# Experts of a mixture-of-experts layer taken four at a time instead of two at a time

## The chip, the cores and the metric

The kernel runs on one core of one Trainium2 chip. The metric is the device time of one launch in microseconds (us). Before the change the median of three runs is 1275.25 us (1270.68 to 1278.07). The engines are TensorE (PE; PEld is its weight load), VectorE (DVE), ScalarE (ACT), GpSimd (POOL) and SyncE (SP), which here only issues transfers.

## The reference, cut to what matters

384 tokens (128 context, 256 latent) pass two layers, each a token mixer (attention, then a long convolution) and a mixture of 32 experts. The experts are what the change touches:

```python
g_idx = argmax(t @ wg + bg)                     # one of 4 groups
e_val, e_idx = top_k(logits of its 8 experts, 2)  # two experts per token
combine = one_hot(expert_id) * weight           # 384 x 2 = 768 (token, expert) rows
a, b = t @ w_gate[e], t @ w_up[e]               # 1024 -> 256
out += (silu(a) * b * combine[e]) @ w_down[e]   # 256 -> 1024
```

All is float32. An expert has 3 MB of weights (gate and up 1 MB each, down 1 MB), a layer 96 MB. Only the rows that an expert was chosen for have to be computed. Counted from the reference on the inputs of the measurement, the experts 0 to 31 get these many rows:

- layer 0: 7 16 1 26 | 18 0 27 11 | 25 5 33 24 | 71 21 11 80 | 13 1 15 55 | 18 28 9 7 | 32 29 55 60 | 14 7 26 23.
- layer 1: 76 24 2 47 | 19 54 2 2 | 51 13 27 20 | 44 31 8 12 | 19 20 4 13 | 27 32 26 25 | 31 4 21 32 | 23 17 25 17.

## The kernel before

**Expert stage.** A layer's 32 experts are taken as 16 pairs. 128 slots stand on the partitions: 64 for one expert of the pair, 64 for the other (`WIN = 64`). In order, a pair does this: its 128 token rows are brought to `G` by an indirect DMA of POOL (the first two pairs: by matrix products with a 0/1 matrix, L825), PE turns them (L832) into `GT`, whose halves ACT (L1207) and DVE (L1627) copy out of the banks; PE multiplies with gate and up (`gate_up`, L849: 8 steps over the inner dimension, 2 experts each, every product 64 stationary columns against 512 moving ones, so that two stand side by side in the array); ACT takes silu (L1230), DVE the weighted product (L1655); PE turns it (L855), DVE copies it (L1658), and PE multiplies with down (L863). ACT (L1238) and DVE (L1667) copy the result to `Y`, and POOL scatters its rows to memory (L1811). In the trace one product stands as two MATMUL records.

**Further windows.** Where an expert of a pair has more than 64 rows, the pair is computed again for slots 65 to 128 and so on (`extra`, L869 to L892 on PE): every engine loads two counts into registers, compares and branches; if there is a window, the whole chain (turn, gate and up, silu, turn, down, copy, scatter) runs through serially, ahead of the pair's first window. By the counts above three pairs have one: experts 12/13 (71), 14/15 (80) in layer 0, 0/1 (76) in layer 1. That is 32 + 3 = 35 passes.

**Weights.** The 12 MB `ring` holds two pairs of 6 MB, each of three 2 MB transfers (gate, up, down). SP issues gate and up of pair q+2 when `gate_up` of pair q has ended (semaphore `gu_mm`, which also follows the pair's further windows) and down when the down product has ended (`dn_mm`).

**Filter work.** During layer 0's experts the kernel also computes the filters of the next mixer, one of eight per two pairs: PE products `taps` (L582), `spectra` (L599 to L604) and `sizes` (L613), written out by hand between the products of the pairs, with copies on DVE and ACT, sums on POOL (L1872), small loads by SP (L391 to L394) and a 768 KB store by ACT for each.

After the last scatter SP loads all expert rows back (L429), and the residual sum and the norm follow.

## Time and profile before

| | us |
|---|---|
| median of 3 runs (lowest, highest) | 1275.25 (1270.68, 1278.07) |
| the profiled execution's own time | 1280.37 |
| its span, first to last instruction | 1278.5 |
| PE busy | 1089.1 (85%) |
| DVE, ACT, POOL busy | 476.8, 257.0, 185.4 |
| moved by DMA | 324.54 MB |

Busy time counts a stretch once however many matrix products overlap in it; the mean of one record is longer than its share of the busy time where products stand side by side. The experts of layer 0 run from about 315 to 627 us of the span, those of layer 1 from about 970 to 1239 us.

### The profile page before, as it was taken

The numbers are of one execution on the slowest core, as the hardware profiler recorded it, in microseconds if no ns is written. First come the engines' busy times: TensorE is split into PE (matmuls) and PEld (weight loads), VectorE is DVE, ScalarE is ACT, GpSimd is POOL, SyncE is SP. The second block draws the span as 40 slices with busy tenths as digits, with TensorE's granted clock in tenths as the row PEclk, the third lists the DMA queues.
The fourth block names the chain that finished last, engine by engine and source line by source line (L and its number), as shares of the span: only waits on it lengthen the run. The fifth ranks groups of instructions, "written<-read, shape, count | busy, mean of one in ns | idle before, by whom it ended". The sixth has DMA issues, their size and how long they took to land.

```text
span 1278.5 us, 14637 instructions
## 1 busy us (share of the span) xinstructions
PE 1089.1 (85%) x5429; PEld 574.4 (45%) x5429; DVE 476.8 (37%) x1014; ACT 257.0 (20%) x498; POOL 185.4 (15%) x209
## 2 busy tenths in 40 slices
PE   5799888987999789999879999989765988878864
PEld 3344555555444234443345565658662422222223
DVE  3355556234233113332263336784540111111116
ACT  2211334022333123223231110000221000000001
POOL 1020000002322023221100002130011222222100
PEclk8899989986999899999889999999967989889997
DMA  9996985532899569999870200505320899999943
GB/s 351 404 322 264 251 294 225 227 132 70 313 395 401 228 238 356 398 406 410 305 286 1 99 1 0 230 1 198 154 94 20 325 413 413 413 412 407 407 161 129
DMA packets 94241, 324.54 MB, mean 254 GB/s; under 512 B 17647, under 2 KB 33423, under 8 KB 77380
## 3 DMA queue, kind: packets, MB, share of 16 engines
q1 hardware_dynamic: 71936, 303.49, 61.3%
q0 software_dynamic: 15504, 13.37, 3.4%
q10 hardware_dynamic: 6708, 6.45, 1.4%
q8 instruction: 58, 0.95, 0.3%
q14 instruction: 35, 0.29, 0.1%
HBM read 333.22 MB, written 30.11 MB: 284 GB/s over the span
## 4 chain that ended last, share of the span: by engine, by line
PE 63%; DMA 19%; DVE 7%; issue 4%; ACT 3%; SPq 3%; POOL 0%; ACTq 0%; another core or an unknown queue 0%; POOLq 0%; DVEq 0%
PE bank L849 15%; DMA ring<-in_moe_w_up 10%; PE bank L997 10%; PE bank L863 6%; PE bank L668 3%; PE bank L1036 3%; PE bank L784 3%; DMA ring<-in_w_ada 3%; DMA hT<-in_hy_log_decay 3%; PE bank L564 3%; PE bank L599 2%; PE bank L1025 2%; PE bank L983 2%; DMA ring<-in_moe_w_down 2%; PE bank L796 2%
## 5 line engine op out<-in xcount | busy, mean ns | idle before, releaser
L849 PE MATMUL bank<-ring,work 128*64 128x512 f32 x1120 | 267.5, 633 | 44.3 <-issue 38.2
L849 PEld LDWEIGHTS bank<-ring,work 128*64 128x64 f32 x1120 | 82.5, 145 | 220.6 <-issue 216.4
L863 PE MATMUL bank<-ring,work 128*64 128x512 f32 x560 | 129.4, 604 | 4.3 <-DVE work L1643 1.5
L997 PE MATMUL bank<-hT,ring 128*128 128x384 f32 x384 | 128.0, 494 | 5.3 <-ACT hT L1134 5.3
L1655 DVE SCALAR_TENSOR_TENSOR work<-bank,work 128x256 f32<-128x256 f32 x32 | 15.5, 484 | 261.3 <-ACT work L1230 248.6
L997 PEld LDWEIGHTS bank<-hT,ring 128*128 128x128 f32 x384 | 74.0, 194 | 58.0 <-issue 9.7
L863 PEld LDWEIGHTS bank<-ring,work 128*64 128x64 f32 x560 | 37.5, 138 | 74.1 <-issue 63.4
L1230 ACT ACTIVATE work<-bank 128x256 f32<-128x256 f32 x32 | 12.3, 383 | 249.8 <-PE bank L849 249.8
L1667 DVE COPY work<-bank 128x512 f32<-128x512 f32 x32 | 22.1, 692 | 106.8 <-PE bank L863 106.8
L1806 POOL DMA_INDIRECT work<-token_vectors,work x28 | 28.7, 1026 | 199.6 <-PE bank L832 185.7
L564 PE MATMUL bank<-ring,condS 128*32 128x256 f32 x768 | 48.6, 408 | 10.0 <-DVE ada L1334 5.5
L1811 POOL DMA_INDIRECT expert_rows<-work x32 | 32.0, 1000 | 114.9 <-DVE work L1667 113.0
L599 PE MATMUL bank<-hT,const 128*128 128x256 f32 x160 | 43.8, 409 | 4.6 <-DVE hT L1365 4.6
L1036 PE MATMUL bank<-work,ring 128*128 128x128 f32 (+1 forms) x256 | 42.2, 327 | 1.7 <-DVE work L1757 1.7
L668 PE MATMUL bank<-hT,ring 128*64 128x384 f32 x256 | 43.0, 489 | 0.0
L784 PE MATMUL bank<-work,ring 128*128 128x384 f32 x128 | 41.5, 487 | 0.7 <-DVE work L1499 0.7
L1270 ACT ACTIVATE work<-bank,pc 128x128 f32<-128x128 f32 (+1 forms) x48 | 17.6, 418 | 119.8 <-PE bank L997 119.8
L1238 ACT ACTIVATE work<-bank 128x512 f32<-128x512 f32 x32 | 19.1, 598 | 111.5 <-PE bank L863 111.5
L1036 PEld LDWEIGHTS bank<-work,ring 128*128 128x128 f32 x256 | 38.4, 190 | 5.5 <-issue 2.1
L1729 DVE TENSOR_SCALAR work<-work,pc 128x385 f32<-128x385 f32 x24 | 11.5, 480 | 76.6 <-ACT work L1270 76.6
L1125 ACT ACTIVATE sq<-xT 128x384 f32<-128x384 f32 x38 | 19.7, 522 | 100.9 <-DVE xT L1421 59.2
L564 PEld LDWEIGHTS bank<-ring,condS 128*32 128x32 f32 x768 | 24.8, 116 | 33.4 <-DVE ada L1334 9.0
(269 smaller groups left out, 1481.5 us busy)
## 6 DMA issues: line engine op xcount, KB each, us to landing
ring<-in_moe_w_gate SPq DMA_DIRECT2D x32, 2048.0 KB
ring<-in_moe_w_up SPq DMA_DIRECT2D x32, 2048.0 KB
ring<-in_moe_w_down SPq DMA_DIRECT2D x32, 2048.0 KB
ring<-in_w_ada SPq DMA_DIRECT2D x24, 2048.0 KB, 12.5
ring<-in_hy_w_in SPq DMA_DIRECT2D x6, 2048.0 KB, 20.4
filter_spectra<-work ACTq DMA_DIRECT2D x8, 768.0 KB
work<-expert_rows SPq DMA_DIRECT2D x16, 384.0 KB, 6.7
ring<-filter_spectra SPq DMA_DIRECT2D x2, 3072.0 KB, 12.1
```

The costliest lines, as they stand in the source:

```text
L564: last = mm(ada_bank(t)[32 * j:32 * j + 32, 0:256], condS[:, 4 * hk + k, :], w[:, k, 256 * j:256 * j + 256], start=(hk == 0 and k == 0), s ...
L599: last = mm(dst, m[:, off:off + P], smdf[:, part if part < 2 else r, c, :], start=(j == 0), stop=(j == len(ops) - 1))
L668: last = mm(bank[m % 2][b * HD:(b + 1) * HD, 0:T], wq[:, k, h * HD:(h + 1) * HD], hT[:, k, :], start=(k == 0), stop=(k == KD - 1))
L784: last = mm(bank[m % 2][:, 0:T], wo[:, k, m * P:(m + 1) * P], oT[:, k, :], start=(k == 0), stop=(k == KD - 1))
L796: last = mm(bank[c][:, 0:NG + NE], hT[:, k, c * P:(c + 1) * P], rout[:, l, k, :], start=(k == 0), stop=(k == KD - 1))
L849: last = mm(bank[2][WIN * j:WIN * (j + 1), :], gt[:, k, WIN * j:WIN * (j + 1)], gu[:, :, j, k, :], start=(k == 0), stop=(k == KD - 1))
L863: last = mm(bank[b + hf][WIN * j:WIN * (j + 1), :], AT[:, k, WIN * j:WIN * (j + 1)], dn[:, j, k, hf * HALF:(hf + 1) * HALF], start=(k == 0 ...
L983: last = mm(b[:, :], m[:, off:off + P], ztok[o][:, c, hf * HALF:(hf + 1) * HALF], start=(j == 0), stop=(j == len(ops) - 1))
L997: last = mm(bank[n % 2][:, 0:T], w[:, k, (n % 4) * P:(n % 4 + 1) * P], hT[:, k, :], start=(k == 0), stop=(k == KD - 1))
L1036: last = mm(bank[4 + m % 2][:, lo:hi], wout[:, k, m * P:(m + 1) * P], st[:, 2, k, a0:a1], start=(k == 0), stop=(k == KD - 1))
L1806: ind(out=G[:, q % 2, :], out_offset=None, in_=hD, in_offset=at_rows(tab[:, 4 * q + 1:4 * q + 2]), bounds_check=T - 1, oob_is_err=False).t ...
L1811: ind(out=yD, out_offset=at_rows(tab[:, 4 * q:4 * q + 1]), in_=Y[:, q % 2, :], in_offset=None, bounds_check=2 * T - 1, oob_is_err=False).t ...
```

## The change

The experts are taken as 8 quads of four, with 32 slots for each (`WIN = 32`). A product now has 32 stationary columns, and four stand side by side. The ring holds one quad in six units of 2 MB: gate and up of the first half of the inner dimension (units 0, 1), gate and up of the second half (2, 3), and the two inner halves of down (4, 5). SP issues units 0 to 3 of quad q+1 when PE has turned the activation of quad q (`at_mm`), units 4 and 5 when PE has turned the token rows of quad q+1 (`gt_mm`). A quad has a further window for each 32 rows, or part of 32, that its fullest expert has beyond 32. Up to two of them (`WOVEN = 2`) are woven in: their gate/up products stand between those of the first window and the turn of its activation, their down products after its down product. More than two would run in a serial loop (`rare`) ahead of the quad. The single buffers `G` and `Y` take the place of double ones.

By the counts, the quads of layer 0 have 0 0 1 2 1 0 1 0 further windows, those of layer 1 have 2 1 1 1 0 0 0 0: ten, and none goes to `rare`. That is 16 + 10 = 26 passes.

```diff
-PAIRS = NE // 2
-WIN = 64
+QUAD = 4
+QUADS = NE // QUAD
+WIN = P // QUAD
+WOVEN = 2
...
         def moe_loads(sp, l):
...
-            for q in range(2, PAIRS):
-                sp.wait_ge(S_("gu_mm"), B_("gu_mm") + q - 1)
-                load_gu(sp, l, q)
-                sp.wait_ge(S_("dn_mm"), B_("dn_mm") + 2 * (q - 1))
-                load_dn(sp, l, q)
-                if l == 0 and q % 2 == 1:
-                    load_filter(sp, q // 2)
+            for q in range(1, QUADS):
+                sp.wait_ge(S_("at_mm"), B_("at_mm") + q)
+                for i in range(4):
+                    load_unit(sp, l, q, i)
+                sp.wait_ge(S_("gt_mm"), B_("gt_mm") + 2 * (q + 1))
+                if l == 0:
+                    load_filter(sp, q)
+                for i in (4, 5):
+                    load_unit(sp, l, q, i)
...
+                def gate_up(gt, half):
+                    gu = half_gu(half)
+                    for k in range(KD // 2):
+                        kk = 4 * half + k
+                        for j in range(QUAD):
+                            last = mm(bank[2][WIN * j:WIN * (j + 1), :], gt[:, kk, WIN * j:WIN * (j + 1)], gu[:, :, j, k, :],
+                                      start=(kk == 0), stop=(kk == KD - 1))
+                    return last
...
+                def extra_gate_up(q):
+
+                    apart(pe)
+                    lo, hi = window_counts(q)
+                    with pe.If(hi > lo):
+                        pe.wait_ge(S_("xgath"), 16 * (lo + 1))
+                        turn_extra(0).then_inc(S_("xgt_mm"), 1)
+                        pe.wait_ge(S_("xgt_set"), 2 * (lo + 1))
+                        pe.wait_ge(S_("act_set"), B_("act_set") + q + 1)
+                        gate_up(GTx, 0)
+                        gate_up(GTx, 1).then_inc(S_("xgu_mm"), 1)
+                        apart(pe)
+                        with pe.If(hi > lo + 1):
...
-                for q in range(PAIRS):
-                    s = q % 2
-                    pe.wait_ge(sem(f"gu_in_{s}"), B_("gu_in") + 32 * (q // 2 + 1))
-                    copied(q)
...
+                for q in range(QUADS):
+                    pe.wait_ge(S_("gta_set"), B_("gta_set") + q + 1)
+                    pe.wait_ge(S_("gtb_set"), B_("gtb_set") + q + 1)
                     if q >= 1:
                         pe.wait_ge(S_("act_set"), B_("act_set") + q)
...
+                    rare(q)
+                    apart(pe)
+                    pe.wait_ge(sem("half_in0"), B_("half_in0") + 32 * (q + 1))
+                    gate_up(GT, 0)
+                    if l == 0 and q >= 1:
+                        for part in range(3):
+                            spectra(q - 1, part)
+                    pe.wait_ge(sem("half_in1"), B_("half_in1") + 32 * (q + 1))
+                    gate_up(GT, 1).then_inc(S_("gu_mm"), 1)
+                    extra_gate_up(q)
                     pe.wait_ge(S_("act_set"), B_("act_set") + q + 1)
-                    turn_act(S_("at_mm"))
+                    turn_act(A, S_("at_mm"))
+                    if l == 0:
+                        taps(q, 0)
+                        taps(q, 1)
...
+                    for hf in range(2):
+                        down(hf).then_inc(S_("dn_mm"), 1)
+                    if l == 0:
+                        taps(q, 2)
+                    extra_down(q)
+                    if q + 1 < QUADS:
+                        pe.wait_ge(S_("gath"), B_("gath") + 16 * (q + 1))
+                        for half in range(2):
+                            gather_turn(half)
+                    if l == 0 and q >= 1:
+                        sizes(q - 1)
```

On POOL, `extra_scatter(q)` waits until each further window's rows have landed before it goes on, and `extra_gather(q+1)` stands behind it; ACT and DVE got `extra_turned`, `extra_silu`, `extra_act` and `extra_rows`, each with its own loads of the two counts and its branch.

PE before, in layer 0: a pair's check (loads of `cumx`, compare), its further window, then the start of the pair's own work. L881 turns the window's rows, L849 is gate/up, L855 the turn of the activation, L863 down.

```order
L870 TENSOR_LOAD cumx
L870 ISA x2
L871 TENSOR_LOAD cumx
L871 ISA x2
L872 COMPARE_AND_BRANCH
L878 UNCONDITIONAL_BRANCH
L878 ISA
L881 MATMUL bank<-const,work 128x128 x8
L883 REGISTER_ALU
L849 MATMUL bank<-ring,work 64x512 x16
L855 MATMUL bank<-const,work 128x128 x2
L863 MATMUL bank<-ring,work 64x512 x8
```

PE after, in a quad of layer 0: the second half of the quad's own gate/up (L844), the check, two further windows (L862 turns rows), and only then the turn of the quad's activation (L850), whose semaphore lets SP load.

```order
L844 MATMUL bank<-ring,work 32x512 x16
L866 TENSOR_LOAD cumx
L866 ISA x2
L867 TENSOR_LOAD cumx
L867 ISA x2
L898 COMPARE_AND_BRANCH
L899 ISA
L862 MATMUL bank<-const,work 128x128 x8
L901 REGISTER_ALU
L844 MATMUL bank<-ring,work 32x512 x32
L906 COMPARE_AND_BRANCH
```

The further window went from ahead of the pair, where it was a chain to the end, to a place inside the quad; its down product moved behind the quad's own.

SP before, in layer 0, the loads of two pairs and the small loads of a filter:

```order
L399 DMA ring<-in_moe_w_gate 128x2x2048
L399 DMA ring<-in_moe_w_up 128x2x2048
L404 DMA ring<-in_moe_w_down 128x4x1024
L399 DMA ring<-in_moe_w_gate 128x2x2048
L399 DMA ring<-in_moe_w_up 128x2x2048
L404 DMA ring<-in_moe_w_down 128x4x1024
L391 DMA hT<-in_hy_log_decay 128x256
```

SP after, one quad:

```order
L408 DMA ring<-in_moe_w_gate 128x4x1024
L408 DMA ring<-in_moe_w_up 128x4x1024
L408 DMA ring<-in_moe_w_gate 128x4x1024
L408 DMA ring<-in_moe_w_up 128x4x1024
L397 DMA hT<-in_hy_log_decay 128x256
L399 DMA sq<-in_hy_filt_w 64x256
L400 DMA sq<-in_hy_filt_b 1x256
L397 DMA hT<-in_hy_log_decay 128x256
L399 DMA sq<-in_hy_filt_w 64x256
L400 DMA sq<-in_hy_filt_b 1x256
L413 DMA ring<-in_moe_w_down 128x4x1024 x2
```

The bytes are the same; 8 MB now start at one point and 4 MB at another, where six points stood for 12 MB, and a run of gate or up is 4 KB long where it was 8 KB.

DVE after, in a quad: the weighted product (L1731), then the check, and behind it the copy of the further window's turned rows (L1728).

```order
L1731 SCALAR_TENSOR_TENSOR work<-bank,work 128x256
L1723 TENSOR_LOAD cumx
L1723 ISA x2
L1724 TENSOR_LOAD cumx
L1724 ISA x2
L1757 COMPARE_AND_BRANCH
L1758 REGISTER_ALU
L1728 COPY work<-bank 128x512
L1731 SCALAR_TENSOR_TENSOR hd<-bank,work 128x256
```

Before, DVE made its check ahead of everything of the pair; now one stands between the product and the copy.

## Rows read from the trace of the kernel before

**Rows 1.** Windows: stretch, its length, busy us and instructions by engine, clock, DMA share, GB/s.
```profile
325.00:601.00 276.00, 260.00 (x1215) 111.89 (x1215) 81.34 (x119) 77.28 (x112) 68.62 (x77) 0.99 0.91 354
488.00:575.00 87.00, 86.83 (x407) 38.13 (x408) 29.51 (x42) 26.12 (x36) 27.08 (x29) 1.00 1.03 398
996.00:1227.00 231.00, 192.72 (x876) 69.92 (x876) 33.91 (x60) 23.32 (x44) 45.06 (x56) 0.93 1.00 404
```

**Rows 2.** Page: groups of instructions, busy us, mean ns of one, idle before.
```profile
L849 PE MATMUL bank<-ring,work 128*64 128x512 f32 x1120 | 267.5, 633 | 44.3 <-issue 38.2
...
L863 PE MATMUL bank<-ring,work 128*64 128x512 f32 x560 | 129.4, 604 | 4.3 <-DVE work L1643 1.5
...
L1655 DVE SCALAR_TENSOR_TENSOR work<-bank,work 128x256 f32<-128x256 f32 x32 | 15.5, 484 | 261.3 <-ACT work L1230 248.6
...
L1230 ACT ACTIVATE work<-bank 128x256 f32<-128x256 f32 x32 | 12.3, 383 | 249.8 <-PE bank L849 249.8
L1667 DVE COPY work<-bank 128x512 f32<-128x512 f32 x32 | 22.1, 692 | 106.8 <-PE bank L863 106.8
```

**Rows 3.** Timeline of PE: start, us, operation; 32-column products, one after an idle stretch.
```profile
27.02 3.66 PE L564 MATMUL bank<-ring,condS 128*32 128x256 f32 x64
36.77 5.57 PE L564 MATMUL bank<-ring,condS 128*32 128x256 f32 x64 [4.36 <-DVE ada L1334]
```

**Rows 4.** Timeline of PE, gate/up of pairs 3, 5, 6, 7 in layer 0.
```profile
367.30 7.09 PE L849 MATMUL bank<-ring,work 128*64 128x512 f32 x32
...
400.66 7.09 PE L849 MATMUL bank<-ring,work 128*64 128x512 f32 x32
...
438.54 7.09 PE L849 MATMUL bank<-ring,work 128*64 128x512 f32 x32 [1.02 <-DVE work L1646]
...
473.42 7.09 PE L849 MATMUL bank<-ring,work 128*64 128x512 f32 x32 [1.01 <-DVE work L1646]
```

**Rows 5.** Timeline, all engines, around the first check of layer 0.
```profile
308.22 0.31 DVE L1609 CAST cumx<-work 1x17 int32<-1x17 f32 x1
...
310.06 1.28 ACT L1230 ACT_TABLE_LOAD   x1 [2.04 <-issue]
```

**Rows 6.** Timeline of PE, first and last passes of the two layers.
```profile
314.92 9.89 PE L849 MATMUL bank<-ring,work 128*64 128x512 f32 x32 [4.85 <-issue]
...
621.34 5.15 PE L863 MATMUL bank<-ring,work 128*64 128x512 f32 x16 [0.52 <-DVE work L1658]
...
944.37 7.63 PE L825 MATMUL bank<-work 128*128 128x128 f32 x48 [3.70 <-DVE work L1579]
969.78 1.96 PE L881 MATMUL bank<-const,work 128*128 128x128 f32 x8 [17.77 <-DMA work<-token_vectors,curx]
...
1047.17 8.99 PE L849 MATMUL bank<-ring,work 128*64 128x512 f32 x32 [5.29 <-issue]
...
1235.52 3.65 PE L863 MATMUL bank<-ring,work 128*64 128x512 f32 x16 [0.52 <-DVE work L1658]
```

**Rows 7.** Timeline of SP: the first load of each layer's loop.
```profile
324.85 0.38 SPq L399 DMA_DIRECT2D ring<-in_moe_w_gate  x1
...
995.11 0.37 SPq L399 DMA_DIRECT2D ring<-in_moe_w_gate  x1
```

**Rows 8.** Timeline of POOL: gathers, and the instruction that waits for their landing.
```profile
443.46 1.04 POOL L1829 DMA_INDIRECT work<-token_vectors,curx  x1 [0.87 <-POOL curx L1826]
445.89 0.19 POOL L1837 COPY curx<-work 128x4 int32<-128x4 int32 x1 [1.40 <-DMA work<-token_vectors,curx]
...
966.31 1.01 POOL L1839 DMA_INDIRECT work<-token_vectors,curx  x1 [0.77 <-POOL curx L1837]
...
996.34 1.02 POOL L1839 DMA_INDIRECT work<-token_vectors,curx  x1 [0.78 <-POOL curx L1837]
1004.60 0.19 POOL L1837 COPY curx<-work 128x4 int32<-128x4 int32 x1 [7.25 <-DMA work<-token_vectors,curx]
```

**Rows 9.** Page: DMA issues, KB each, median us to landing (two in flight).
```profile
ring<-in_w_ada SPq DMA_DIRECT2D x24, 2048.0 KB, 12.5
```

More of the change, by code:

```diff
@@ L326, in build @@
         mtmp = [small(2, TC, NE) for _ in range(3)]
-        posk, rowk, wck, basek, wink, rowq = [small(2, TC) for _ in range(6)]
+        posk, rowk, wck, basek, wink = [small(2, TC) for _ in range(5)]
         idx = sb("idx", [P, TC * 2], I32)
@@ L438, in further @@
             return nc.s_assert_within(at, 0, top,
-                                      skip_runtime_bounds_check_because="a count is at most 384, so a window is at most 5")
+                                      skip_runtime_bounds_check_because="a count is at most 384, so a window is at most 11")
         def apart(eng):
@@ new lines, in turn_act, with down @@
+                def turn_act(act, done):
+                    for k in range(2):
+                        last = tr(bank[3][:, k * P:(k + 1) * P], act[:, k * P:(k + 1) * P], ident)
+                    last.then_inc(done, 1)
+                def down(hf):
+                    for k in range(2):
+                        for j in range(QUAD):
+                            last = mm(bank[4 + hf][WIN * j:WIN * (j + 1), :], AT[:, k, WIN * j:WIN * (j + 1)],
+                                      unit_dn(k)[:, j, hf * HALF:(hf + 1) * HALF], start=(k == 0), stop=(k == 1))
+                    return last
@@ L921, in moe @@
                     if q >= 1:
                         pe.wait_ge(S_("y_set"), B_("y_set") + 2 * q)
-                    down(s, 4, S_("dn_mm"))
-                    if l == 0 and q % 2 == 1:
-                        taps(q // 2, 2)
-                    if l == 0 and q % 2 == 0 and q >= 2:
-                        spectra(q // 2 - 1, 2)
-                        sizes(q // 2 - 1)
+                    for hf in range(2):
+                        down(hf).then_inc(S_("dn_mm"), 1)
+                    if l == 0:
+                        taps(q, 2)
@@ new lines, in moe @@
+                for q in range(QUADS):
+                    rare(q)
+                    extra_gather(q)
+                    apart(pool)
+                    if q + 1 < QUADS:
+                        if q >= 1:
+                            pool.wait_ge(S_("gt_mm"), B_("gt_mm") + 2 * (q + 1))
+                        gather(G, record(0, q + 1, 1), S_("gath"))
+                    if l == 0 and q >= 1:
+                        size_sums(q - 1)
+                    pool.wait_ge(S_("y_set"), B_("y_set") + 2 * (q + 1))
+                    scatter(Y, record(0, q, 0), S_("scat"))
+                    extra_scatter(q)
+                    apart(pool)
```

602 lines of the change are left out of this document (336 added, 266 removed).

## The prediction, written before the run

> **What bounds the kernel now.** I read the windows first. From 488 to 575 us, in the experts of layer 0, PE is busy 86.83 of 87 us and the DMA moves 398 GB/s at full share [rows 1]: both are bound. Over all of the stage the DMA reaches 354 GB/s at a share of 0.91, so it has holes. The gate/up passes show where: two pairs follow each other by 33.4 us (367.30 to 400.66), but pairs 5 to 7, between which two further windows run, need 72.8 us instead of 33.4, which is 39.4 us lost [rows 4]. In layer 1 the DMA is at share 1.00 for 231 us, while PE is busy 193 of them [rows 1]: there only the transfers count, from the first load at 995.11 [rows 7] to the last byte at 1227, and a tail of 12.2 us to the end of the last down product at 1239.2 (1235.52 + 3.65) [rows 6]. So the stage must be priced by when loads can start and how long the DMA is dry, not by PE time.
>
> **Matrix work.** A pass of gate/up costs 7.09 us warm [rows 4], down 3.65 [rows 6]; 35 passes make the 267.5 and 129.4 us of busy time [rows 2]. With four 32-column products side by side a pass would cost the same, and 26 would be left: 9 x 10.7 = 96 us of PE time less. The nearest rows are 32-column products of 256: 64 records (32 products) in 3.66 us [rows 3]. A quad's gate/up has 32 products of 512, so 7.3 us by that row; I take 7.1. These 96 us are no gain by themselves, since the DMA is bound beside them.
>
> The Trainium skill (TensorE: Matmul & The Clock Gate, Part 3: Packing small matmuls) says that three column tiles measured 2.38x, not 3x. By that efficiency (estimate from the page: 3.2x for four) gate/up would cost some 1.8 us more a pass and down 0.9, and the sum below 29 us more. The row of 3.66 us speaks against it: it is what one of four products would need for the whole count; nothing of the overlap is missing there.
>
> **Transfers.** The bytes stay. Layer 0 from the second quad on: 7 x 12.58 MB of weights, filters 7 x 0.39, stored spectra 7 x 0.79, rows in and out 5.8, together 102.1 MB, at 398 GB/s 256.5 us, 36.6 a quad. Layer 1: 231 us, 33.0 a quad. I cost the shorter runs (4 KB for 8) at nothing; down is loaded so already, within a stretch at 404 GB/s [rows 1]. Start and landing of a load together cost 2.3 us (12.5 for two units, less 10.2) [rows 9].
>
> **When the DMA runs dry.** Loads of the next quad now wait for the turn of the activation, behind all further windows. When the second half of gate and up has landed, only the two down units are still on their way: 10.4 us in layer 1, 13.5 in layer 0 with the filter loads and a store. Against it stands a chain on PE, ACT and DVE. Its parts: second half of gate/up 3.5; silu 0.4, weighting 0.5 and the copy of the window's turned rows 0.7 [rows 2], with a check of counts between, for which I take 1.5 (ACT from the counts at 308.53 to its next instruction at 310.06 [rows 5]), so 3.2 with semaphores; a window's gate/up 7.1; turn 0.5 (eight turns 1.96 at half clock [rows 6]).
>
> Without a window: 2.3 + 3.5 + 1.0 + 0.5 = 7.3 us, under 10.4: no gap. With one, in layer 0: 2.3 + 3.5 + 3.2 + 7.1 + 0.5 = 16.6, gap 3.1, for quads 2 and 6. In layer 1 PE idles ahead of each half, and after 5.29 us of idling a pass took 8.99 instead of 7.09 [rows 6]; so 1.9 more: 18.5, gap 8.1, for quads 2 and 3.
>
> Quad 3 of layer 0 (one window before it, two of its own) is bound by PE. A quad's own PE work is the 33.4 us of two pairs less one pass and one set of turns, 21.8. To it come two gate/up 14.2, the previous window's down 3.65, and serial waits: 3.3 ahead of that down (copy, filter copy, check, copy), 1.0 behind it, 3.2 for the copies and check ahead of the first half (the first quad's 4.85 [rows 6] bounds it), 2 x 3.2 at the windows. Together 53.5, gap 17. Quad 4 (two before, one own): 21.8 + 7.1 + 7.3 + 3.3 + 2.9 + 3.2 + 3.2 = 48.8, gap 12. Layer 0: 3 + 3 + 17 + 12 = 35 us dry.
>
> Quad 1 of layer 1 (two before, one own) is bound by POOL, which waits for each landing. A gather lands in 8.3 us beside the weights (996.34 to 1004.60), in 2.4 to 3.4 with the DMA idle (443.46 to 445.89; 966.31, and PE goes on at 969.78) [rows 6, 8]. The scatters' landing under load is not shown; bounds 2.4 and 8.3, taken 8, as the gather's. From the turn: down, copy, check, copy, the window's down and copy 11.4; scatter 8; scatter 8; two checks 3; gather 8; turn cold 2.0, copy 0.8, gate/up 9.0, turn 0.5: 50.7, gap 17.7. Layer 1: 17.7 + 2 x 8.1 = 34 us dry.
>
> **The sum.** Layer 0: gate/up of the first quad ends at 324.8 as before [rows 6], the turn at 326.4, bytes from 327.4 on; + 256.5 + 35 = 618.9 for the last byte; landing 1.3 and down 3.65 make 623.9. Before, down ended at 626.5 [rows 6]: the two serial windows of 39.4 are gone, and PE no longer has two pairs left when the last byte lands, but the dry stretches eat it: -2.6. Layer 1: turns of the first gather end at 952.0, and 4.85 + 9.89 later [rows 6] gate/up at 966.7; the first window's rows land about 967.9 (POOL 3.3 us earlier by two gathers and a copy, 1.5 later by a check), then 1.1 + 0.8 + 7.1 + 3.2 + 7.1 + 0.5 lead to 987.7, bytes from 988.8 instead of 996: -7.2. Dry: +34. Tail 5.5 instead of 12.2: -6.7. Layer 1: +20. All else (norms, long convolution, residual) shifts along; the loads for the convolution are issued 40 us before their use. Sum +17.5; as the DMA is dry when quad 1's last gather runs, its landing is nearer 3.4, so I take +14.5. The profiled execution is 1280.37 us, span 1278.5, 5 over the median; the difference is set on the median 1275.25: **1290 us**.
>
> **Rivals.**
> 1. The dry stretches are small and the end of the serial windows wins (faster). Checks are hidden by the queues (-1.5 at four windows, -4.5 at quad 3, -3 at quad 4: -13.5), POOL's landings take 3.4 (quad 1's gap falls to its neighbours', -11), halves run warm (-5.7): 17.5 - 30 = -12.5, 1263 us. For: PE shows no idle time at checks in 488 to 575. Against: these checks stood ahead of work that was already queued; the new ones stand behind a semaphore. It decides where all dry stretches together stay under 51 us instead of 69.
> 2. Gaps also at quads without a window in layer 1, and dearer checks. Cold the chain is 2.3 + 7.1 + 1.0 + 0.9 + a check of 2.2 = 13.5 against 10.4: 3 quads x 3.1; and up to 1.5 more at each of seven quads with a window: +19, 1309 us. For: 1047.17 [rows 6] and PE's 44% of work in layer 1. Against: a clock grant comes back within such a pass, and the check may run beside the half pass. The Trainium skill (TensorE: Matmul & The Clock Gate, HAM oscillation) has it that each burst behind an idle stretch starts at 1.2 GHz; the row agrees with it for that pass.
> 3. The four products do not overlap fully, so the change does not do what it says: +29 on top, 1319 us. Only the row at 36.77 (5.57 us, after 4.36 idle) looks like it, and that is the clock.
>
> **Numbers.** The forecast 0.50 (1275 to 1302), rival 1 0.23, rival 2 0.22, rival 3 0.05. About 0.5% (6.4 us) is what a measurement of this kernel can tell from no change. Faster: most of rival 1, 0.19. Within 0.5%: the rest of it and the low end of the forecast, 0.15. Slower: 0.66. The range 1264 to 1310 leaves out 0.2.
>
> **What would show it.** Gate/up about 7.1 us for 64 records warm. In layer 1 the DMA share below 0.2 for 14 to 18 us in quad 1 and some 8 in quads 2 and 3, none in quads 4 to 6. Layer 0's last down within 5 us of 626; layer 1's stage (first load to last down) 271 us instead of 244. PE's busy time some 80 to 100 us lower, less what the lower clock takes back. The prediction is wrong if the DMA stays at full share beside a further window, or if layer 0 ends over 10 us earlier.

## The result and the profile after

The change makes the kernel slower: 1317.86 us (median of 4 runs, 1313.1 to 1324.37) against 1276.19 before (4 runs), a ratio of 1.0337 with a 95% interval of 1.0282 to 1.0393, +41.7 us. The forecast was 1290 with a range of 1264 to 1310. The sign was right; the size forecast, 14.5 us, is a third of what came.

Both profiled executions, in us, cut at the same four points (SP's first load of each loop, the end of the last down product of each layer). Their spans differ by 44.1 us, as the changed kernel's profiled execution (1324.37 us) is the slowest of its four; the forecast's terms add up to 17.5, of which it took 14.5:

| | before | after | change | forecast |
|---|---|---|---|---|
| start to first load of layer 0 | 324.9 | 324.8 | 0 | 0 |
| first load to last down, layer 0 | 301.6 | 318.3 | +16.7 | -2.6 |
| from there to the first load of layer 1 | 368.6 | 360.7 | -7.9 | -7.2 |
| first load to last down, layer 1 | 244.1 | 277.4 | +33.3 | +27.3 |
| from there to the end | 39.3 | 41.3 | +2.0 | 0 |

The page of the changed kernel, first the shares of PE and the packets, then the groups that answer to [rows 2]:

```profile
PE 1024.2 (77%) x6075; PEld 527.4 (40%) x6075; DVE 447.9 (34%) x968; ACT 239.4 (18%) x469; POOL 128.4 (10%) x125
...
DMA packets 103598, 325.07 MB, mean 246 GB/s; under 512 B 10544, under 2 KB 26384, under 8 KB 103092
...
L844 PE MATMUL bank<-ring,work 128*32 128x512 f32 x1664 | 238.5, 725 | 111.8 <-DMA ring<-in_moe_w_up 68.8
...
L856 PE MATMUL bank<-ring,work 128*32 128x512 f32 x832 | 111.6, 685 | 37.1 <-DVE work L1734 19.0
```

PE works 64.9 us less and idles more: ahead of gate/up 111.8 us, of which 68.8 end with the landing of weights; before it was 44.3, of which 38.2 are "issue" [rows 2], idle time for which the profile shows no cause. The 68.8 us are not the loss: q_none below, which is faster, waits 127.5 us for weights. Nearly all packets are now under 8 KB (103092 of 103598; before 77380 of 94241). The windows that answer to [rows 1] (the columns are the same), the stage of layer 0, that of layer 1, and its last three quads, which have no further window:

```profile
325.00:633.00 308.00, 236.89 (x1529) 92.92 (x1527) 65.63 (x104) 73.04 (x103) 41.23 (x37) 0.88 0.87 330
1004.00:1272.00 268.00, 165.52 (x1126) 48.85 (x1126) 25.26 (x45) 16.97 (x32) 21.09 (x21) 0.83 0.89 348
1155.00:1272.00 117.00, 65.40 (x382) 18.12 (x382) 7.34 (x13) 5.12 (x10) 6.02 (x6) 0.79 1.01 397
```

In layer 1 the DMA is dry for a tenth of the time, and in the last three quads, at a mean share of 1.01, it moves 397 GB/s where the stage of before had 404. In windows of 3 us one sees the hole of quad 1, here its lowest part:

```profile
1038.00:1041.00 3.00, 0.00 (x0) 0.00 (x0) 0.00 (x0) 0.00 (x0) 0.00 (x0) 0.50 0.23 90
1041.00:1044.00 3.00, 2.06 (x12) 1.67 (x16) 0.69 (x1) 0.60 (x1) 1.01 (x1) 0.50 0.03 5
...
1047.00:1050.00 3.00, 3.00 (x28) 0.80 (x24) 0.00 (x0) 0.00 (x0) 0.00 (x0) 0.82 0.00 0
```

Adding up what each such window lacks to a share of 1, the holes are (forecast behind them): layer 0, quads 2, 3, 4, 6: 7.7 (3.1), 14.5 (17), 15.0 (12), 6.0 us (3.1), together 43 (35); layer 1, quads 1, 2, 3: 14.8 (17.7), 7.8 (8.1), 9.0 us (8.1), together 32 (34). The timeline of PE in quad 2 of layer 0 shows the chain that the prediction added up, from the second half of gate/up to the turn that lets SP load:

```profile
393.25 3.64 PE L844 MATMUL bank<-ring,work 128*32 128x512 f32 x32 [0.38 <-DMA ring<-in_moe_w_up]
396.82 1.09 PE L862 MATMUL bank<-const,work 128*128 128x128 f32 x8
399.64 7.07 PE L844 MATMUL bank<-ring,work 128*32 128x512 f32 x64 [1.73 <-DVE work L1728]
406.64 0.44 PE L850 MATMUL bank<-const,work 128*128 128x128 f32 x2
```

13.9 us from 393.25 to SP's load at 407.11; the forecast had 14.3 for it. The 64 records of a full pass take 7.07 us, as the 32 records of a pair's pass took 7.09 [rows 4], so the four 32-column products overlap as fully as the two of 64 columns did.

Not in the forecast: the two tails. The last quad of layer 0, and below it the last of layer 1:

```profile
629.51 0.33 PE L850 MATMUL bank<-const,work 128*128 128x128 f32 x1 [1.04 <-DVE work L1731]
...
633.38 0.47 PE L850 MATMUL bank<-const,work 128*128 128x128 f32 x1 [3.54 <-issue]
633.64 3.62 PE L586 MATMUL bank<-sq,hd 65*128 65x512 f32 x4
...
637.20 5.95 PE L856 MATMUL bank<-ring,work 128*32 128x512 f32 x32
...
1272.07 0.44 PE L850 MATMUL bank<-const,work 128*128 128x128 f32 x2 [1.03 <-DVE work L1731]
1275.14 6.12 PE L856 MATMUL bank<-ring,work 128*32 128x512 f32 x32 [2.63 <-issue]
```

In layer 0 PE stands 3.54 us between two turns though the profile shows nothing to wait for, and the filter products come next. Down takes 5.95 and 6.12 us instead of 3.65 [rows 6]: PE has just idled, and the granted clock is 0.50, its lower level (1.2 GHz), from 634 to 638 us, and 0.59 on average, so mostly that level, from 1275 to 1281.3.

### The profile page after: what moved, and what is told of

It is laid out like the page before. It is cut to its first block, busy times and chain, and to the rows that moved or that the text cites. A ratio compares the mean times of both kernels' runs of the same rounds, so it can differ in the third digit from the quotient of the medians.

```text
span 1322.6 us, 16585 instructions
## 1 busy us (share of the span) xinstructions
PE 1024.2 (77%) x6075; PEld 527.4 (40%) x6075; DVE 447.9 (34%) x968; ACT 239.4 (18%) x469; POOL 128.4 (10%) x125
## 2 busy tenths in 40 slices
DMA packets 103598, 325.07 MB, mean 246 GB/s; under 512 B 10544, under 2 KB 26384, under 8 KB 103092
## 4 chain that ended last, share of the span: by engine, by line
PE 53%; DMA 28%; DVE 6%; issue 5%; SPq 3%; ACT 2%; DVEq 1%; POOLq 1%; another core or an unknown queue 0%; POOL 0%; ACTq 0%
DMA ring<-in_moe_w_up 18%; PE bank L844 11%; PE bank L1046 10%; PE bank L672 3%; PE bank L1085 3%; PE bank L788 3%; DMA expert_rows<-work 3%; DMA ring<-in_w_ada 3%; PE bank L856 3%; PE bank L568 3%; PE bank L1074 2%; PE bank L1032 2%; DMA work<-token_vectors,work 2%; PE bank L603 2%; PE bank L800 2%
## 5 line engine op out<-in xcount | busy, mean ns | idle before, releaser
L844 PE MATMUL bank<-ring,work 128*32 128x512 f32 x1664 | 238.5, 725 | 111.8 <-DMA ring<-in_moe_w_up 68.8
L844 PEld LDWEIGHTS bank<-ring,work 128*32 128x32 f32 x1664 | 61.6, 130 | 265.1 <-issue 172.1
L856 PE MATMUL bank<-ring,work 128*32 128x512 f32 x832 | 111.6, 685 | 37.1 <-DVE work L1734 19.0
L856 PEld LDWEIGHTS bank<-ring,work 128*32 128x32 f32 x832 | 28.4, 123 | 108.8 <-issue 82.7
L1731 DVE SCALAR_TENSOR_TENSOR work<-bank,work 128x256 f32<-128x256 f32 x16 | 7.7, 484 | 177.2 <-ACT work L1320 177.2
L1954 POOL DMA_INDIRECT expert_rows<-work x26 | 26.1, 1004 | 401.1 <-DVE work L1804 313.1
L568 PE MATMUL bank<-ring,condS 128*32 128x256 f32 x768 | 48.6, 407 | 10.2 <-DVE ada L1428 5.5
L603 PE MATMUL bank<-hT,const 128*128 128x256 f32 x160 | 41.4, 409 | 5.3 <-DVE hT L1459 5.3
L1466 DVE COPY work<-bank 128x512 f32<-128x512 f32 x16 | 11.1, 692 | 98.0 <-PE bank L603 92.9
L1320 ACT ACTIVATE work<-bank 128x256 f32<-128x256 f32 x16 | 6.1, 383 | 209.5 <-PE bank L844 209.5
L1950 POOL DMA_INDIRECT work<-token_vectors,work x24 | 24.5, 1021 | 159.4 <-issue 148.3
L603 PEld LDWEIGHTS bank<-hT,const 128*128 128x128 f32 x160 | 30.7, 200 | 19.0 <-issue 9.7
L568 PEld LDWEIGHTS bank<-ring,condS 128*32 128x32 f32 x768 | 24.8, 117 | 33.8 <-DVE ada L1428 9.0
L1869 DVE TENSOR_SCALAR work<-work,pc 128x385 f32<-128x385 f32 x24 | 11.5, 480 | 75.4 <-ACT work L1364 75.4
## 6 DMA issues: line engine op xcount, KB each, us to landing
ring<-in_w_ada SPq DMA_DIRECT2D x24, 2048.0 KB, 12.6
```

The costliest lines, as they stand in the source:

```text
L568: last = mm(ada_bank(t)[32 * j:32 * j + 32, 0:256], condS[:, 4 * hk + k, :], w[:, k, 256 * j:256 * j + 256], start=(hk == 0 and k == 0), s ...
L603: last = mm(dst, m[:, off:off + P], smdf[:, part if part < 2 else r, c, :], start=(j == 0), stop=(j == len(ops) - 1))
L844: last = mm(bank[2][WIN * j:WIN * (j + 1), :], gt[:, kk, WIN * j:WIN * (j + 1)], gu[:, :, j, k, :], start=(kk == 0), stop=(kk == KD - 1))
L856: last = mm(bank[4 + hf][WIN * j:WIN * (j + 1), :], AT[:, k, WIN * j:WIN * (j + 1)], unit_dn(k)[:, j, hf * HALF:(hf + 1) * HALF], start=(k ...
L1954: ind(out=yD, out_offset=at_rows(at), in_=src, in_offset=None, bounds_check=2 * T - 1, oob_is_err=False)\
```

## The experiments

**1. What do the windows cost, what the rest?** Four kernels separate them: quads without windows, with and without the windows' code, and pairs the same way.

```diff
-                link(v.tensor_scalar(c1[:, 0, 1:NQ], big, float(WOVEN), None, ALU.min))
-                link(v.tensor_scalar(c1[:, 1, 1:NQ], big, float(WOVEN), 0.0, ALU.subtract, ALU.max))
+                link(v.tensor_scalar(c1[:, 0, 1:NQ], big, 0.0, None, ALU.min))
+                link(v.tensor_scalar(c1[:, 1, 1:NQ], big, 64.0, 0.0, ALU.subtract, ALU.max))
```

> The changed kernel with every quad's count of further windows set to 0: the code for them stays and is jumped over, the rows beyond 32 of an expert are not computed (the row buffer in memory is filled once from the token vectors, 3 MB ahead of layer 0's experts, where the DMA has room). Theory A: the loss is the DMA lying dry while the further windows still need the ring. The dry stretches that the changed kernel's windows show are 8, 15, 16 and 7 us in layer 0 (46) and some 34 in layer 1, and the first load of layer 1 comes 17 us later than the end of the first gate/up allows. All of it goes: 1318 - 46 - 51 = about 1220 us, a quad's loads 36 to 37 us apart in layer 0, 33 to 34 in layer 1. Rival B: checks, jumps and the shorter runs of the loads cost at every quad, windows or not: 1235 us or more, with dry stretches of 2 us or more in every quad.

Measured: 1228.4 us (0.9632 of before, 0.9612 to 0.9652), between the two theories. The ten windows cost 89.5 us, 9.0 each. The medians of the kernel before, taken beside each group of runs, lie between 1273.7 and 1276.2 us, so a single term below is good to some 2 us.

For q_nocode the calls go as well:

```diff
-                    rare(q)
-                    extra_gate_up(q)
-                    extra_down(q)
```
(and their like on ACT, DVE and POOL)

> As q_none, and the code of the further windows (checks, branches, the loop for more than two) is taken out of all engines as well. In the changed kernel PE stands idle 2.6 to 4.8 us with nothing to wait for behind the branch over a further window that isn't there. Theory A: these stalls lie beside the transfers but for the two tails (3.5 + 2.6), the two starts (4.4 + 5.8) and 1 to 2 us at some quads of layer 0: 8 to 16 us less than q_none. Rival: the stalls are PE waiting for the silu and the copies, not for code; then 0 to 3 us less, and the idle time behind the turn of the activation stays.

Measured: 1212.0 us, 16.4 less than q_none, at the upper end of theory A; but my reason for the stalls was wrong in part. Without a branch in the program PE still idles ahead of a quad's down product, though nothing that the profile shows holds it:

```profile
1025.06 0.44 PE L853 MATMUL bank<-const,work 128*128 128x128 f32 x2 [1.03 <-DMA ring<-in_moe_w_down]
1028.34 5.34 PE L859 MATMUL bank<-ring,work 128*32 128x512 f32 x32 [2.84 <-issue]
```

Most of the 16.4 us lies at the two starts. The first gate/up of layer 0 comes behind 2.46 us of idling, in q_none behind 5.81; from the first rows' products to the first load it is 19.0 us in q_nocode and 24.9 in q_none (layer 1: 20.6 and 24.5). q_8k (experiment 4), with the same code up to there as q_nocode, has its first load 3.2 us later, so one start alone is known to some 3 us. The Trainium skill (Runtime: NRT & Kernel Launch, Instruction fetch mechanics) says that a taken branch whose target lies outside the fetched pages stalls for a fetch. The starts agree with it; the 2.84 us of the row above, behind no branch, are not explained by it and stay open.

```diff
+                link(v.tensor_scalar(c1[:, 1:PAIRS + 1], c1[:, 1:PAIRS + 1], 0.0, None, ALU.mult))
```

> The kernel before the change with the counts of further windows set to 0, code kept, rows beyond 64 of an expert not computed, row buffer filled as in q_none. Layer 0 loses its 39 us of serial windows but is bound by the DMA then (97.7 MB at 400 GB/s = 245 us from 326, plus a tail of 12 to 16): last down at 590 to 600 instead of 626.5, and layer 1's first load comes 27 us earlier. Theory A: 1276 - 30 - 27 = about 1219, within 8 us of q_none: without windows four at a time is neither better nor worse, so the change's effect is all in how the windows are run. Rival B (quads are slower in themselves): p_none is 15 us or more below q_none. Rival C (quads are faster in themselves and only the windows spoil it): q_none is 10 us or more below p_none.

Measured: 1216.9 us (0.9541, 0.9522 to 0.9560). So the three serial windows of pairs cost 58.7 us, 19.6 each, and quads are 11.5 us behind pairs even without windows: between theory A and rival B. The same without code:

> As p_none (the kernel before without further windows), and the checks and the code of the windows are taken out on PE, ACT, DVE and POOL (POOL's gathers of the second windows stay). For quads that was worth 16.4 us. Theory C1: a check costs alike wherever it stands, and pairs have 32 of it where quads have 48 on PE: about 11 us less, 1206. Theory C2: before the change the checks stand ahead of products that wait for nothing, and two pairs lie in the ring, so a stall of 4 us is made good: 0 to 4 us less, 1213 or more, and then the quads' stalls are a cost that the change brought.

Measured: 1204.3 us, 12.6 less than p_none. C1 holds: pairs pay for their checks too, and the 16.4 us of quads are only 3.8 more.

**2. Is it the ring that the windows hold?** The prediction's picture was that transfers wait behind the windows. q_freed lets them go first; `still_gate_up` reads a resident tile instead of the ring:

```diff
-                        gate_up(GTx, 0)
-                        gate_up(GTx, 1).then_inc(S_("xgu_mm"), 1)
+                        still_gate_up(0)
+                        still_gate_up(1).then_inc(S_("xgu_mm"), 1)
...
-                    extra_gate_up(q)
                     pe.wait_ge(S_("act_set"), B_("act_set") + q + 1)
                     turn_act(A, S_("at_mm"))
+                    extra_gate_up(q)
```

> The changed kernel with all its windows, but their gate/up products read a resident tile of the same width instead of the ring, so that the turn of the quad's activation, which lets SP load, stands ahead of them; PE does the same products. The further windows' rows are wrong, their count and shapes as before. Theory A (the weights are held, PE's work is not the matter): the stretches of the quads with one window go (8, 7, 8, 9), of the quad after one with two windows about 15 us stay in layer 0 and about 12 in layer 1, since PE needs over 50 us there; layer 1's first load comes 17 us earlier: 1318 - 30 - 40 = about 1248 us (1240 to 1258). Rival: PE's work, checks and waits are what costs, wherever the loads are released: 1290 us or more.

Measured: 1350.7 us. The total says little, as layer 1 got other windows from layer 0's wrong rows; but layer 0, whose windows are unchanged, took 326.8 us from first load to last down instead of 318.3, where 30 us less were expected. A quad with one window in layer 1 still took 40.8 us from load to load, as in the changed kernel (41.4). Down's loads still waited for the next quad's turned rows, behind the windows. q_free2 fixes the windows' counts and releases down early too:

```diff
-                link(v.tensor_scalar(big, big, BIG, 0.0, ALU.subtract, ALU.max))
+                link(v.memset(big, 0.0))
+                for i, n in enumerate(((0, 0, 1, 2, 1, 0, 1, 0), (2, 1, 1, 1, 0, 0, 0, 0))[l]):
+                    if n:
+                        link(v.memset(big[:, i:i + 1], float(n)))
...
-                            down(hf).then_inc(S_("xdn_mm"), 1)
+                            still_down(hf).then_inc(S_("xdn_mm"), 1)
...
-                sp.wait_ge(S_("gt_mm"), B_("gt_mm") + 2 * (q + 1))
+                sp.wait_ge(S_("dn_mm"), B_("dn_mm") + 2 * q)
```

> Nothing of the ring is held for a further window any more: its gate/up and its down read a resident tile of the same width, SP may load gate and up once the quad's own activation is turned and down once its own down product has ended (in q_freed down still waited for the next quad's turned rows, behind the windows, and in layer 1 the wrong rows had changed the number of windows; here the counts are constants, those of the changed kernel, in both layers). The windows' rows are wrong, PE's, DVE's, ACT's and POOL's work is the same. Theory P (PE's chain of a quad with a window, about 41 us in layer 1 and 48 in layer 0, is longer than the quad's transfers, so releasing the ring earlier gives nothing in those quads; only the start of layer 1, where loads wait for two windows, gains some 16 us): 1295 to 1308 us. Theory A (the prediction's: the transfers wait behind the window, and would fill the gap if they could start): the dry stretches of 46 + 34 us shrink to those of the quads after two windows, 1265 us or less.

Measured: 1326.2 us, 8 us more than the changed kernel. Theory A (1265 or less) is far off, but theory P (1295 to 1308) is missed by 18 us as well. The 16 us at layer 1's start came (75.2 us instead of 91.4 from the first rows' products to the second quad's end, 977.09 to 1052.28; 3 of them are a shorter idle time ahead of the first gate/up, 2.66 us for 5.76), but layer 0 now took 336.6 us from first load to last down instead of 318.3. The waits of PE in layer 0's stage (engine, line, waited for: us, times, longest), first of the changed kernel:

```profile
PE bank L844 <- DMA ring<-in_moe_w_up: 23.7, 7, 8.4
PE bank L844 <- issue: 8.9, 4, 3.8
PE bank L850 <- issue: 8.4, 2, 4.8
PE bank L856 <- DVE work L1734: 7.8, 5, 1.8
PE bank L844 <- DVE work L1728: 6.8, 5, 1.8
```

and of q_free2:

```profile
PE bank L844 <- issue: 16.4, 6, 4.5
PE bank L586 <- issue: 10.2, 3, 7.2
PE bank L844 <- DMA ring<-in_moe_w_up: 10.0, 4, 4.2
PE bank L927 <- DVE work L1754: 7.8, 5, 1.8
PE bank L850 <- DVE work L1751: 7.3, 7, 1.0
PE bank L862 <- issue: 4.9, 4, 1.3
```

The windows of the same stage, the changed kernel's and then q_free2's (PE's busy time is the second number):

```profile
324.80:634.00 309.20, 237.71 (x1532) 93.57 (x1531) 65.74 (x105) 74.02 (x105) 41.23 (x37) 0.87 0.87 329
```

```profile
319.20:639.00 319.80, 253.21 (x1531) 96.48 (x1530) 65.42 (x104) 70.13 (x99) 41.10 (x37) 0.85 0.84 319
```

The waits for weights fell from 23.7 to 10.0 us, as intended. In their place came 10 us more of "issue" (31.5 for 21.6), and PE is busy 253.2 us instead of 237.7: the same products take longer at a mean granted clock of 0.85 instead of 0.87. One quad of layer 1 with one window shows where PE now idles:

```profile
1051.81 0.44 PE L850 MATMUL bank<-const,work 128*128 128x128 f32 x2 [1.02 <-DVE work L1751]
1053.47 1.96 PE L862 MATMUL bank<-const,work 128*128 128x128 f32 x8 [1.22 <-issue]
1056.22 9.07 PE L899 MATMUL bank<-xT,work 128*32 128x512 f32 x64 [0.78 <-DVE work L1748]
1066.68 3.64 PE L856 MATMUL bank<-ring,work 128*32 128x512 f32 x32 [1.39 <-DVE work L1754]
1070.26 0.44 PE L850 MATMUL bank<-const,hd 128*128 128x128 f32 x2
1072.37 3.64 PE L927 MATMUL bank<-xT,work 128*32 128x512 f32 x32 [1.68 <-DVE work L1754]
1077.35 1.09 PE L836 MATMUL bank<-const,work 128*128 128x128 f32 x8 [1.33 <-DVE work L1796]
1083.24 9.21 PE L844 MATMUL bank<-ring,work 128*32 128x512 f32 x64 [4.80 <-issue]
```

From turn to turn (1051.81 to 1093.47) this quad takes 41.7 us with no wait for weights in it: 29.5 of products and 12.2 of short waits. The transfers of a quad need 33. So with the ring free PE's chain is the longer one.

But part of that chain was made by the edit. With the quad's own turn ahead of the window, PE waits for the activation (1.02 us) and idles once more (1.22) before it can turn the window's rows. From the end of the quad's own gate/up to its down product it is 15.9 us here (1050.79 to 1066.68) and 13.0 in the next quad. The changed kernel turns the window's rows while the activation is being made; its quad 3 of layer 1 needs 11.3 us (1127.17 to 1138.45):

```profile
1127.17 1.09 PE L862 MATMUL bank<-const,work 128*128 128x128 f32 x8
1130.00 7.07 PE L844 MATMUL bank<-ring,work 128*32 128x512 f32 x64 [1.73 <-DVE work L1728]
...
1138.45 3.64 PE L856 MATMUL bank<-ring,work 128*32 128x512 f32 x32 [1.01 <-DVE work L1734]
```

Another 4.80 us are the idle time ahead of gate/up, which the changed kernel has too. Without the loop `rare` (q_norare, experiment 3) it is gone, and quad 2 of layer 1 shows what then holds it:

```profile
1052.32 3.64 PE L844 MATMUL bank<-ring,work 128*32 128x512 f32 x32 [1.22 <-DMA ring<-in_moe_w_up]
1063.12 5.84 PE L844 MATMUL bank<-ring,work 128*32 128x512 f32 x32 [7.17 <-DMA ring<-in_moe_w_up]
...
1071.71 7.07 PE L844 MATMUL bank<-ring,work 128*32 128x512 f32 x64 [1.72 <-DVE work L1726]
1078.72 0.44 PE L850 MATMUL bank<-const,work 128*128 128x128 f32 x2
```

SP's loads at 1038.33 and at 1079.19 are 40.9 us apart: 24.8 until the second half is there, 16.1 for its pass, the window and the turn. PE waits 8.4 us of it for weights, so its own chain needs 32.5. Here the loads that wait behind the window set the quad, as the prediction had it (33.0 + 8.1). In the changed kernel PE waits 2.1 and 6.7 us for weights in quads 2 and 3 of layer 1, so the two chains lie close together there. What an early release with PE's order kept would be worth, no run shows.

**3. Products or waits?** q_short cuts a window's products and leaves the rest:

```diff
-                        gate_up(GTx, 0)
-                        gate_up(GTx, 1).then_inc(S_("xgu_mm"), 1)
+                        short_gate_up(0)
+                        short_gate_up(1).then_inc(S_("xgu_mm"), 1)
...
-                            down(hf).then_inc(S_("xdn_mm"), 1)
+                            short_down(hf).then_inc(S_("xdn_mm"), 1)
```

> The changed kernel in which a further window's gate/up has 8 products instead of 32 and its down 8 instead of 16 (their results are wrong, and so that layer 1 has the same windows the counts are written in as constants: 0 0 1 2 1 0 1 0 and 2 1 1 1 0 0 0 0). All checks, turns, copies, gathers and scatters stay. PE has 10 x (5.3 + 1.8) = 71 us less to do. Theory P (q_freed showed that the turn-to-turn time of a quad with one window is 41 to 49 us wherever the loads are released, so PE's own chain sets it): most of it comes back until a quad is down at its transfers, 1318 - 55 = 1250 to 1270 us. Theory W (not the products but the waits between them, the checks and the landings of gathers and scatters make a window dear): 1285 us or more.

Measured: 1264.5 us (ten runs, 1259.1 to 1271.7), 53.4 less than the changed kernel, in the range of theory P: of 71 us of products three quarters lay on the path. It doesn't tell the two chains apart, since a window's gate/up stands in both. The quads of layer 1 with one window take 36.4 and 36.7 us from load to load instead of 41.4 and 42.6, though PE waits 8.5 us for weights in the second of them.

q_pool takes POOL's wait for the landing of a window's scatter out (ACT and DVE got it instead):

```diff
                         scatter(Yx[:, 0, :], record(1, q, 0), S_("xscatter"))
-                        pool.wait_ge(S_("xscatter"), 16 * (lo + 1))
                         apart(pool)
```

> The changed kernel, all computed, but POOL no longer waits until a further window's scattered rows have landed; ACT and DVE wait for that before they next write Yx, and POOL once behind the last quad. In the trace of the changed kernel PE waits 8.0 us for a gather in quad 1 of layer 1, 2.9 in quad 4 of layer 0, 1.4 and 1.0 in two others, and each such gather is issued behind two landings of 6 to 8 us. Prediction's term (POOL's chain sets quad 1 of layer 1, and the landings under load are what make it): 8 to 12 us less, 1306 to 1310. Rival: PE's own chain is only just shorter than POOL's there, 0 to 4 us less.

Measured: 1305.4 us, 12.4 less: POOL's landings were on the path as said, most of it in layer 1 (from first load to last down 267.6 us for 277.4).

q_norare drops the call `rare(q)` on four engines:

> The changed kernel without the loop for more than two further windows of a quad (rare) and without its two counts, comparison and branch, on PE, ACT, DVE and POOL; no quad here has more than two, so what is computed stays. All checks and branches together were worth 16.4 us where no window runs (q_none less q_nocode). Theory C (PE stands still behind each branch over code that isn't run, and the loop is the longer of the two pieces): half of it or more comes back, 1305 to 1310 us. Rival: in quads with windows the check stands beside transfers that are waited for anyway, 1315 or more.

Measured: 1305.2 us, 12.7 less, theory C. PE's waits for weights ahead of gate/up rose from 68.8 to 91.6 us: a part of the stalls only turned into those. Both together:

> The changed kernel without the loop rare and with POOL not waiting for the landing of window scatters (q_norare and q_pool in one), all computed. Each gave back 12.5 us. If they lie in different places (a check at every quad, POOL's chain in quad 1 of layer 1 and quad 4 of layer 0), they add up: 1291 to 1296 us. If both shorten the same waits in the quads with windows: 1299 or more. In both cases slower than before the change.

Measured: 1295.5 us (1.0129, 1.0086 to 1.0172). 22.3 us of 25.1 add up, and with both repairs it is still slower than before.

**4. The shorter runs.** The prediction took nothing for them.

```diff
-                cols = slice(half * (KD // 2) * EH, (half + 1) * (KD // 2) * EH)
-                src = a[...][l, QUAD * q:QUAD * (q + 1)].rearrange("j (p k) h -> p j (k h)", p=P)
-                sp.dma_start(half_gu(half)[:, u].rearrange("p j k h -> p j (k h)"), src[:, :, cols])\
+                two = QUAD * q + 2 * half
+                src = a[...][l, two:two + 2].rearrange("j (p k) h -> p j (k h)", p=P)
+                sp.dma_start(half_gu(half)[:, u].rearrange("p (j a) k h -> p j (a k h)", a=2), src)\
```

> As q_nocode (quads, no windows, no checks), but a unit of gate or up holds two experts whole in runs of 8 KB, where it holds half the inner dimension of four in runs of 4 KB; the same bytes at the same points (products get other weights). q_nocode is 7.8 us above p_nocode, 1212.0 against 1204.3. If the shorter runs cost (the prediction took nothing), 5 to 8 us come back: 1204 to 1207. If not (one quad in the ring, starts behind the turn of the activation), 1210 or more.

Measured: 1200.6 us, 11.4 less than q_nocode, more than the 5 to 8 foreseen and than the whole distance to pairs. Windows of layer 1, first the stretch and then two of the lowest windows of 3 us in it, q_nocode and then q_8k:

```profile
925.00:1150.00 225.00, 121.27 (x696) 33.35 (x688) 15.14 (x26) 10.66 (x20) 13.07 (x13) 0.75 0.99 391
1024.00:1027.00 3.00, 0.47 (x6) 0.20 (x2) 0.91 (x2) 0.38 (x1) 0.00 (x0) 1.00 0.63 213
1093.00:1096.00 3.00, 0.44 (x2) 0.20 (x2) 0.42 (x1) 0.00 (x0) 0.00 (x0) 0.73 0.64 172
```

```profile
925.00:1140.00 215.00, 111.76 (x674) 31.09 (x672) 14.79 (x26) 10.07 (x19) 13.07 (x13) 0.79 1.00 407
985.00:988.00 3.00, 0.44 (x2) 0.20 (x2) 0.42 (x1) 0.00 (x0) 0.00 (x0) 1.00 0.81 280
1084.00:1087.00 3.00, 1.10 (x8) 0.46 (x12) 0.16 (x1) 0.00 (x0) 0.00 (x0) 0.67 0.79 251
```

Over the stretch the rate is 391 GB/s against 407, 4%, with runs of 4 KB instead of 8 KB in two thirds of the bytes. Only part of it is the rate of a busy DMA: the windows of 3 us with a share of 0.99 or more move 409 GB/s in q_nocode (63 of 75) and 416 in q_8k (64 of 71), 1.7% apart. The rest are the dips at the change from one quad to the next, like those shown. Measured against the share of 1.02 that such full windows have, they make up 6.9 us in q_nocode and 2.7 in q_8k. Why they are smaller with the other layout is not shown.

The Trainium skill (DMA: Bandwidth & Descriptors, Why small descriptors are slow) gives an overhead of about 3 cycles for each packet, beside what becomes 128 beats for 4 KB, and 32 bytes of description for each operation; by that, an estimate from the page, halving the runs costs some 1.6% of the halved part and 1% of all. The 1.7% of the full windows is near it; the 4% of the stretch is not explained by it.

**5. A version that beats both.** The woven window is worth having, the small one isn't. p_weave puts it into the pairs:

```diff
                     gate_up(GT, s, S_("gu_mm"))
+                    lo, hi = extra_gate_up(q)
                     if q + 1 < PAIRS:
                         gathered(q + 1, 0)
+                    extra_down(q, lo, hi)
```

with `extra` gone from its place ahead of the pair, and SP's loads of gate and up waiting for `gu_free`, which PE raises behind the window. POOL gathers only where there is a window and no longer waits for its scatter. It runs at most one window of a pair, enough for experts of up to 128 rows (here 80).

> The kernel before the change (pairs, 64 slots, ring of two pairs), but with its further window woven in as the change does it for quads: its gate/up behind that of the pair's own, its activation turned and its down product done just ahead of the pair's own, scatter not waited for, gathered only where there is one. It runs one further window of a pair (up to 128 rows of an expert; the most here are 80) and gives all of the reference. Without windows pairs take 1216.9, with three serial ones 1275: 19.5 us each, the one of pair 0 in layer 1 some 27 as PE waits 17.8 us for its gather ahead of everything. Theory (the weaving is good, the small windows are what is dear, since there are ten of them): the PE work of a window is 12.3 us, some of it hidden by transfers, so 3 x 8 to 3 x 12 instead of 58: 1240 to 1253 us. Rival: what a window holds back in the ring costs as much as the serial chain did: 1265 or more.

Measured: 1247.6 us, 0.9771 of before (0.9732 to 0.9810), 70 us below the changed kernel. Its three windows cost 30.7 us over p_none, 10.2 each; how much of the gain over 19.6 is the weaving and how much POOL's part, no run separates. The start of layer 1:

```profile
931.75 7.09 PE L850 MATMUL bank<-ring,work 128*64 128x512 f32 x32 [1.43 <-DVE work L1634]
945.46 1.97 PE L875 MATMUL bank<-const,work 128*128 128x128 f32 x8 [6.62 <-DMA work<-token_vectors,work]
948.21 10.08 PE L850 MATMUL bank<-ring,work 128*64 128x512 f32 x32 [0.78 <-DVE work L1642]
```

The pair's own pass runs while the gather is under way, and PE waits 6.62 us for it instead of 17.77 [rows 6].

## Why the prediction was right and wrong

The 41.7 us by the medians: windows 89.5 for 58.7, +30.8; checks 16.4 for 12.6, +3.8; shorter runs +11.4; what is left of quads against pairs, 1200.6 for 1204.3, -3.7. Sum +42.3. The last three terms were measured without windows. In the prediction's own steps:

- **Matrix work.** Right: 7.07 us a pass. Rival 3 is out, though its 1319 us is the number nearest to the result; that is chance.
- **Layer 1.** The start (-7.9 for -7.2) and the dry stretches (32 us for 34) came as worked out. Its +6 over the forecast are some 4 us of lower rate (397 GB/s for 404 over 231 us) and 3.3 in the tail.
- **Layer 0 is where the sum failed, by 19.3 us.** The step "Transfers: I cost the shorter runs at nothing": outside the holes the stage ran some 262 us for the same bytes that I had put at 256.5, so 5 to 6 us here. That step, some 10 us in both layers with the small dips at the quads' changes in it, is the largest mis-sized term; q_8k measured the layout alone, at 11.4 us without windows. The rows had a hint and I read it past: the stretch at 404 GB/s had one transfer in three in short runs, now it is all.
- **"Then the two down units are still on their way, 13.5 us in layer 0".** In quad 2 the DMA went dry 7.6 us behind the landing of the second half (393.2 to 400.8), in quad 6 9: filter loads, the store and part of down had gone beside the second half and not behind it. That is 3 to 5 us in each of the two quads, and with quad 4 (a window's pass at the lower clock, 9.70 us, and a gather 2.9 us late) the 8 us more of holes.
- **The tails.** 5 us were forecast from the last byte to the end of down in layer 0, it is about 10; 5.5 in layer 1, it is about 9. No row of before showed a check or a cold pass behind the last byte, but 5.29 us of idling and 8.99 for a pass at 1047.17 [rows 6] did show what PE does when it runs short of work; I applied it to halves of gate/up and not to the tail. This term is mis-sized by some 5 us in layer 0 and 3.5 in layer 1.
- **Checks.** The forecast had 1.5 us for one, and only in quads with a window. Rival 2 made them dearer and stood at 1309. Taken out of quads without windows they are worth 16.4 us, the loop that never runs 12.7 in the changed kernel.
- **The mechanism.** Loads that wait behind the windows do set the quads of layer 1 with one window: without the stall at `rare` such a quad takes 40.9 us from load to load while PE waits 8.4 us for weights, and the holes together have the size forecast in layer 1 (32 us for 34). What the prediction did not see is that PE's own chain of products, short waits and stalls is nearly as long. In q_free2, where nothing holds the ring, it came out at 41.7 us where the transfers take 33, though that run's own edit lengthened it. I had used that bound only for quads 3 and 4 of layer 0.

Of the 96 us of PE work that 9 passes less save, 64.9 us show in busy time, as part of the rest runs at the lower clock. They lay beside transfers; what counts is the number of windows and what each adds to its quad: ten at 9.0 us instead of three at 19.6.

## What to carry to other kernels

Halving the tile to save work on sparse rows multiplies the leftovers: count them from real data and multiply by the serial price of one, before counting the passes saved. Before releasing a buffer earlier, measure the compute engine's chain with its waits for the transfer taken out: if it is nearly as long as the hole's cycle, little comes back. And check that the release doesn't put a new wait into that chain, as it did here. Weave the rare path into the large tile first, and take it apart only then.

## What the runs showed of the hardware

- Loads of 2 MB that all have runs of 4 KB move 409 GB/s in windows of full DMA share; with 8 KB in two thirds of them it is 416 (q_nocode, q_8k). Over a whole stretch, with the dips at the quads' changes, it is 391 against 407.
- Code that is never run costs: the loop `rare` 12.7 us of 1318, all checks of a kernel 12.6 to 16.4 us. Ahead of layer 0's first gate/up PE idled 5.81 us with the code in q_none, 4.44 in the changed kernel, and 2.46 without it (q_nocode).
- PE idles 2.4 to 2.8 us ahead of a down product with neither a branch nor a visible wait (q_nocode). Why was not found out.
- Taking away waits for weights can cost as much in clock: in layer 0's stage they fell from 23.7 to 10.0 us, PE's busy time rose from 237.7 to 253.2 (changed kernel, q_free2). Passes behind short waits took 9.07 us (1056.22) and 7.07 (1096.99), both behind idle times of 1.02, 1.22 and 0.78 us; the waits just before do not decide it alone.
